# Queries and keys turned in 32x32 blocks on VectorE and gathered back from DRAM, in a hybrid attention decoder step

## The reference, cut to what matters

```python
h = rms_norm(x, norm_g); z = einsum('bsd,de->bse', h, w_in)     # one combined input projection
qa, ka, va, ga, qb, kb, vb, gb, ma, mb = split(z)
qa = rms_norm(qa per head of 64, q_norm_a); ka = rms_norm(ka, k_norm_a)   # the same for qb, kb
# A: 3 groups (window, dilation) = (128,1), (512,4), (2048,16), 8 heads each
scores = einsum('brnihd,brnjhd->brnhij', q, k) * d ** -0.5 + alibi ; out_g = softmax(scores) @ v
# B: 4 heads, two maps each: (softmax(s1) - lam * softmax(s2)) @ v
# gates, two branch projections, sigmoid merge, output projection, residual
# outputs too: the sampled window caches, shifted by 8 tokens, with the new rows behind
new_a{g}_sample = concat(cache_a{g}[:, 8:], new rows)
```

## Time and profile before

| | |
|---|---|
| Median of 3 runs | 1697.23 us (1694.59 to 1698.11) |
| The profiled execution's own time | 1693.59 us |
| Its span in the trace | 1691.7 us |
| PE busy | 1628.7 us, 96% |
| DVE, ACT, POOL busy | 719.9, 598.9, 665.4 us (43%, 35%, 39%) |
| Queue q1 (SyncE's), q10 (ScalarE's) | 221.68 MB, 112.22 MB |

### The profile page before, as it was taken

The page is one execution under the profiler, slowest core; times in us unless marked ns, Lnnn a source line. Parts: engine busy times, 40 slices in busy tenths (PEclk is TensorE's granted clock), DMA queues, the critical chain, the costliest instruction groups (busy, mean ns, idle before and its releaser), DMA issues.

```text
span 1691.7 us, 37775 instructions
## 1 busy us (share of the span) xinstructions
PE 1628.7 (96%) x14872; PEld 1394.2 (82%) x14872; DVE 719.9 (43%) x1788; ACT 598.9 (35%) x1405; POOL 665.4 (39%) x958
## 2 busy tenths in 40 slices
PE   7999999999999999999999999999899999999998
PEld 5787677878899999999999977788777788878787
DVE  6521576222372221722217544335354342588411
ACT  5422477222362221732218233334343344422300
POOL 5566120467433564535646221212221121565500
PEclk9999999999999999999999999999999999999999
DMA  5164810775516568155442879889898977865422
GB/s 166 54 236 154 260 50 13 229 241 185 180 44 212 191 219 282 43 183 195 155 128 67 298 268 325 276 290 349 262 309 297 323 258 234 285 204 176 135 94 81
DMA packets 184064, 336.30 MB, mean 199 GB/s; under 512 B 29969, under 2 KB 74130, under 8 KB 177746
## 3 DMA queue, kind: packets, MB, share of 16 engines
q1 hardware_dynamic: 143586, 221.68, 40.2%
q10 hardware_dynamic: 40304, 112.22, 19.9%
HBM read 294.05 MB, written 127.07 MB: 249 GB/s over the span
## 4 chain that ended last, share of the span: by engine, by line
PE 79%; DMA 6%; SPq 5%; DVE 3%; issue 3%; ACT 3%; POOL 2%; ACTq 0%; POOLq 0%; DVEq 0%
PE ps L2008 13%; PE ps L2010 13%; PE ps L2009 13%; PE ps L2167 4%; PE ps L2223 4%; PE ps L2065 4%; PE ps L2113 3%; PE ps L2066 3%; PE ps L2067 3%; PE ps L2187 3%; PE ps L2282 2%; DMA v_in<-in_cache_a_kv 2%; PE ps L2174 2%; DMA raw<-in_w_in 2%; PE ps L2134 2%
## 5 line engine op out<-in xcount | busy, mean ns | idle before, releaser
L993 POOL TENSOR_TENSOR w_lo<-raw,w_hi 128x512 fp32r<-128x512 f32 x140 | 181.2, 1300 | 424.2 <-ACT w_hi L1203 423.6
L2008 PE MATMUL ps<-w_hi,hT 128*128 128x512 f32 x824 | 339.6, 412 | 2.1 <-POOL hT L980 1.0
L2010 PE MATMUL ps<-w_hi,hT 128*128 128x512 f32 x824 | 330.1, 401 | 0.0
L2009 PE MATMUL ps<-w_lo,hT 128*128 128x512 f32 x824 | 329.7, 400 | 0.0
L2008 PEld LDWEIGHTS ps<-w_hi,hT 128*128 128x128 f32 x824 | 205.9, 250 | 21.4 <-DVE w_lo L1522 1.5
L2010 PEld LDWEIGHTS ps<-w_hi,hT 128*128 128x128 f32 x824 | 206.0, 250 | 20.3
L2065 PE MATMUL ps<-w_hi,hT 128*128 128x256 f32 x768 | 221.3, 288 | 1.2 <-issue 0.8
L2009 PEld LDWEIGHTS ps<-w_lo,hT 128*128 128x128 f32 x824 | 206.3, 250 | 18.1
L2066 PE MATMUL ps<-w_lo,hT 128*128 128x256 f32 x768 | 214.6, 279 | 1.0 <-issue 0.8
L2067 PE MATMUL ps<-w_hi,hT 128*128 128x256 f32 x768 | 214.1, 279 | 0.0
L1203 ACT ACTIVATE w_hi<-raw 128x512 fp32r<-128x512 f32 x158 | 98.9, 629 | 217.8 <-DMA raw<-in_w_in 198.6
(11 more groups left out here) (233 smaller groups left out, 2852.4 us busy)
## 6 DMA issues: line engine op xcount, KB each, us to landing
out<-in_cache_a_kv ACTq DMA_DIRECT2D x29, 2040.0 KB, 9.8
k_in<-in_cache_b_kv SPq DMA_DIRECT2D x128, 256.0 KB, 4.3
v_in<-in_cache_b_kv SPq DMA_DIRECT2D x128, 256.0 KB, 6.3
raw<-in_w_in SPq DMA_DIRECT2D x104, 256.0 KB, 4.1
k_in<-in_cache_a_kv SPq DMA_DIRECT2D x104, 256.0 KB, 7.0
v_in<-in_cache_a_kv SPq DMA_DIRECT2D x104, 256.0 KB, 7.3
out<-in_cache_a_kv ACTq DMA_DIRECT2D x7, 2016.0 KB, 8.7
raw<-in_w_in ACTq DMA_DIRECT2D x40, 256.0 KB, 5.6
```

The costliest lines, as they stand in the source:

```text
L993: pool.tensor_tensor(lo, raw_of(q), hi.bitcast(F32), ALU.subtract).then_inc(lo_done, 1)
L2008: pe.matmul(z, hi, wh, start=first, stop=False)
L2009: pe.matmul(z, hi, wl, start=False, stop=False)
L2010: return pe.matmul(z, lo, wh, start=False, stop=last)
```

## The change

Prompt queries and keys are no longer transposed on TensorE. VectorE transposes the 32x32 blocks of each tile within `zn` (queries) or from `kn` into `zn` (keys); SyncE stores the tile to a DRAM scratch `blocks_scr` and loads the whole of it back by 16 DMAs for each kind and group (`load_turned`), each of 32 partitions x 32 pieces of 32 floats (128 bytes), so that `qT` and `kT` come out as before. Query loads are issued two in each step of the k block, key loads three in each step of the v block from at_ = 1. Only the 64 sampled queries are still turned by TensorE (one turn in each k block). The score scale is now applied by GpSimd as it fills `qz`, and the register loop is unrolled. The 48 cache copies are all issued by SyncE: none in q and k blocks, 0, 5, 6, 6 in the v blocks (ahead of tile 8), 12, 8, 7, 4 in the attentions; each waits for the landing of the last but one. Their packets are 2048 and 2720 bytes. Some semaphores are shared to stay within their number.

```diff
-COPY_PARTS = ((0, 0, 120, 1536), (1, 0, 504, 1536)) + tuple((2, 510 * j, 510, 2720) for j in range(4))
-COPY_AT = (1, 2, 4, 6, 7)
+COPY_PARTS = ((0, 0, 120, 512), (1, 0, 504, 512)) + tuple((2, 510 * j, 510, 680) for j in range(4))
+COPIES_IN = (12, 8, 7, 4)
+COPIES_V = (0, 5, 6, 6)
...
+        def copied_at(j):
+            return (const_in, N_CONST + 16 * (j // 2 + 1)) if j % 2 else (copies, 16 * (j // 2 + 1))
...
+            def store_blocks(G, kind, i):
+                sp.wait_ge(turned, tile_turned(G, kind, i))
+                sp.dma_start(blocks_scr[G][kind == "k"][i * P:(i + 1) * P, :], zn[:, mi(G, kind, i) % 2, :])\
+                    .then_inc(blocks_sent(G, kind, i)[0], 16)
+            def load_turned(G, kind, part):
+                c, j = divmod(part, 4)
+                if part == 0:
+                    for i in range(NT - 2, NT):
+                        sp.wait_ge(*blocks_sent(G, kind, i))
+                    if kind == "q" and G:
+                        sp.wait_ge(o_out, stored(G - 1))
+                base = blocks_scr[G][kind == "k"][0:1, 0:1]
+                src = bass.AP(base.tensor, base.offset + c * P + 32 * j, [[CW, 32], [32 * CW, SEQ // 32], [1, 32]])
+                out = (kT if kind == "k" else qT)[32 * j:32 * j + 32, c * SEQ:(c + 1) * SEQ]
+                sp.dma_start(out.rearrange("p (b r) -> p b r", r=32), src).then_inc(kt_in if kind == "k" else qt_in, 16)
             def block_io(u):
...
                     if at_ < KC:
                         load_chunk(u + 1, at_)
+                    if kind in "qk" and i:
+                        store_blocks(G, kind, i - 1)
+                    if kind == "k" and i:
+                        for part in range(2 * i - 2, 2 * i):
+                            load_turned(G, "q", part)
+                    if kind == "v" and 0 < at_ < 7:
+                        for part in range(3 * at_ - 3, min(3 * at_, 16)):
+                            load_turned(G, "k", part)
...
+                    if kind == "v" and at_ >= NT - COPIES_V[G]:
+                        j = sum(COPIES_IN[:G]) + sum(COPIES_V[:G]) + at_ - NT + COPIES_V[G]
+                        if at_ < NT:
+                            copies_under_way(j, j + 1)
...
             def tables(G):
+                j0 = sum(COPIES_IN[:G]) + sum(COPIES_V[:G + 1])
+                share = COPIES_IN[G] // (2 if G == 0 else 3)
                 if G == 0:
-                    for j in range(len(COPY_AT)):
-                        copy_cache(sp, len(COPY_AT) + j)
                     for h in range(2, B_HEADS):
+                        copies_under_way(j0 + (h - 2) * share, j0 + (h - 1) * share)
                         sp.wait_ge(bs, 16 + 16 * (h - 1))
                         table_b(h)
...
+            def copies_under_way(j0, j1):
+                for j in range(j0, j1):
+                    if j == 0:
+                        sp.wait_ge(const_in, N_CONST)
+                    if j >= 2:
+                        sp.wait_ge(*copied_at(j - 2))
+                    copy_cache(sp, j)
...
+            def scaled(G, half, i, c):                              # GpSimd
+                rows, cols = slice(HD * half, HD * half + HD), slice(i * P, (i + 1) * P)
+                return pool.tensor_scalar(qz[rows, half, cols], qT[rows, c * SEQ + i * P:c * SEQ + (i + 1) * P],
+                                          qcol[rows, (0 if G else 1):(0 if G else 1) + 1], None, ALU.mult)
             def pad_first(G):
-                pool.wait_ge(t_ready, 17 * G + 17)
+                pool.wait_ge(turned, tile_turned(G, "k", NT - 1))
+                for i in range(NT - 2, NT):
+                    pool.wait_ge(*blocks_sent(G, "k", i))
...
-                pool.wait_ge(t_moved, 17 * G + 9)
+                pool.wait_ge(setup, 1)
+                pool.wait_ge(qt_in, 256 * (G + 1))
...
-                    if u and u != 2 and at_ in COPY_AT and len(COPY_AT) * (u - 1) + COPY_AT.index(at_) < N_COPIES:
-                        copy_cache(act, len(COPY_AT) * (u - 1) + COPY_AT.index(at_))
...
-                    if kind == "q" and i:
-                        move(G, "q", i - 1)
-                    if kind == "k" and i != 1:
-                        move(G, "q", NT) if i == 0 else move(G, "k", i - 2)
-                    if kind == "v" and at_ == 0:
-                        move(G, "k", NT - 1)
+                    if kind == "k" and i == 0:
+                        move(G)                                     # the sampled queries alone
...
+                        if kind == "q" and i < NT:                  # VectorE, behind zn
+                            dve.wait_ge(zn_ready, m + 1)
+                            dve.transpose(zn[:, m % 2, :], zn[:, m % 2, :]).then_inc(turned, 1)
+                        if kind == "k" and i:
+                            kk = TILES * G + i - 1
+                            dve.wait_ge(kn_ready, kk + 1)
+                            dve.transpose(zn[:, (m - 1) % 2, :], kn[:, kk % 3, :]).then_inc(turned, 1)
...
-                    if kind == "q" and i:                           # TensorE
-                        turn(G, "q", i - 1)
-                    if kind == "k" and i != 1:
-                        turn(G, "q", NT) if i == 0 else turn(G, "k", i - 2)
-                    if kind == "v" and at_ == 0:
-                        turn(G, "k", NT - 1)
+                    if kind == "k" and i == 0:
+                        turn_sample(G)
...
                 pe.wait_ge(v_ready, 9 * G + 8)
-                pe.wait_ge(t_moved, 17 * G + 17)
+                pe.wait_ge(t_moved, G + 1)
+                pe.wait_ge(kt_in, 256 * (G + 1))
```

More of the change, by code:

```diff
@@ L316, in build_step @@
         st_scr = [dram(f"st_scr{g}", [SEQ, 16]) for g in range(3)]
+        blocks_scr = [[dram(f"blocks_scr{g}{kind}", [SEQ, CW]) for kind in "qk"] for g in range(4)]
         os_scr = dram("os_scr", [2, DEC_B, ROW_C, P])
@@ L337, in build_step @@
         t_ready, t_moved = sem("t_ready"), sem("t_moved")
+        turned = sem("blocks_turned")
+        turn_out = [sem(f"blocks_out{s}") for s in range(2)]
+        qt_in, kt_in = sem("qT_in"), sem("kT_in")
         k_out = [sem(f"k_out{s}") for s in range(3)]
@@ L381, in build_step @@
         m_ready, m_t, m_hi, m_lo = sem("m_ready"), sem("m_t"), sem("m_hi"), sem("m_lo")
-        xl_in = [sem(f"xl_in{s}") for s in range(2)]
+        X_LOADS = [16 * len(range(s, TILES, 2)) for s in range(2)]
         yo_ready = sem("yo_ready")
@@ L393, in mi, with tile_turned, blocks_sent @@
             return 18 * G + (9 if kind == "k" else 0) + i
-        def ti(G, kind, i):
-            return 17 * G + (9 if kind == "k" else 0) + i
+        def tile_turned(G, kind, i):
+            return 16 * G + (8 if kind == "k" else 0) + i + 1
+        def blocks_sent(G, kind, i):
+            m = mi(G, kind, i)
+            return turn_out[m % 2], 16 * sum(x % 18 % 9 < NT for x in range(m % 2, m + 1, 2))
         def x_bank(j):
@@ L693, in copy_cache @@
             eng.dma_start(dst.rearrange("(m a x) -> a m x", a=16, x=piece),
-                          src.rearrange("(m a x) -> a m x", a=16, x=piece)).then_inc(copies, 16)
+                          src.rearrange("(m a x) -> a m x", a=16, x=piece)).then_inc(copied_at(j)[0], 16)
         block = ctx.enter_context(nc.Block())
@@ L881, in _ @@
                 if gg == -1:
[L882 removed]
+                    sp.wait_ge(first_in, 48)
             def gated(m):
@@ L952, in _ @@
                 sp.wait_ge(yo_out[s], 16 * 6)
-            sp.wait_ge(copies, 16 * N_COPIES)
+            for j in range(N_COPIES - 2, N_COPIES):
+                sp.wait_ge(*copied_at(j))
             for s in range(3):
@@ L1034, in block_ @@
                             G3, i3 = divmod(kk - 3, TILES)
-                            pool.wait_ge(t_ready, ti(G3, "k", min(i3, NT - 1)) + 1)
+                            pool.wait_ge(turned, tile_turned(G3, "k", min(i3, NT - 1)))
                             if k_sent[kk % 3][kk - 3]:
@@ L1068, in pad_queries @@
                             pool.wait_ge(aq, 16 + 64 * (G - 1) + 16 * (c - 1) + 2 * i + 2)
-                            cols = slice(i * P, (i + 1) * P)
-                            src = slice(c * SEQ + i * P, c * SEQ + (i + 1) * P)
-                            copied(qz[0:HD, 0, cols], qT[0:HD, src])
-                            copied(qz[HD:P, 1, cols], qT[HD:P, src]).then_inc(qz_ready, 1)
+                            scaled(G, 0, i, c)
+                            scaled(G, 1, i, c).then_inc(qz_ready, 1)
                     return
-                with pool.Fori(0, NC - 1) as c:
+                for c in range(1, NC):
                     for s, i in enumerate(TILE_ORDER):
-                        wait_reg(pool, bq, 16 + 16 * c + 2 * s + 2)
-                        cols = slice(i * P, (i + 1) * P)
-                        pool.tensor_copy(qz[0:HD, 0, cols], qT[0:HD, ds((c + 1) * SEQ + i * P, P)])
```

(23 more changed lines are left out.)

64 lines of the change are left out of this document (25 added, 39 removed).

## The result

The kernel after takes 1723.83 us (median of 4 runs, 1721.41 to 1727.47) against 1696.82 us for the kernel before (4 runs beside it): a ratio of 1.0152, interval 1.0133 to 1.0171, 27 us or 1.5% slower. The forecast was slower at 1703 us, with a range of 1675 to 1739. The profiled execution took 1722.63 us, its span 1720.6.

A forecast was written before the change was run, and what follows sets the result against it. TensorE, busy for 96% of the span, was taken as the bound. Turns -32, v blocks +37 and k blocks +1 gave +6 on the profiled 1693.6, so 1699.6; on the median 1703 us, range 1675 to 1739.

The forecast's parts named there:

- What it removes: Q and k blocks: sixteen prompt turns a group leave TensorE, 0.45 or 0.55 us each, 32 us in all.
- What it adds at no cost: VectorE's 64 block transposes (43 us) and GpSimd's scaled copies stay hidden; at most 5 us would show in block u = 0.
- The k blocks: Chunk-fetch round with store and query loads takes 11.0 to 11.5 us against 11.2 for two tiles; 1 us on TensorE.
- The v blocks: Key loads, chunks and copies in SyncE's one queue delay keys and last chunk at the A attentions; 37 us on TensorE.
- The prices: DMA in the v blocks: full copy 6.0 us, small copy a quarter, key load 1.1, chunk or 256 KB table 0.7.
- so 37: Start of the A attentions: 40 us of lateness less four units' scores already done, 1 us a group, leaves TensorE 37.
- The lateness: Last chunk of the v blocks against its due time: 6.3, 17.4 and 16.7 us late in G = 1 to 3, 40 summed.
- The credit of 3 us: Start of the A attentions: TensorE has four units' scores done while the last chunk is late, 1 us for each group.
- the forecast's own case: Whole kernel slower by +3.4 to +25 us, 1700.6 to 1722, likeliest 1703; chance 0.35.
- All hidden: V blocks: queue not served in order or chunks come around the copies; -32 + 1, 1666 us; chance 0.08.
- The queue drains faster: V blocks: copies and loads some 9 us shorter over three groups; -22 to -3.4 us, middle 1684; chance 0.27.
- Small packets dear: V-block loads at the upper end or the 512-byte price, 1.9 us each; over +25 us, middle 1739; chance 0.17.

The follow-up runs named there:

- e2: Kernel after, but the 48 copies as in the kernel before (large packets, in the blocks, on ScalarE's queue, five by SyncE in G = 0): 1768.97 us, ratio 1.0408.
- e10: Kernel after with four copies in each v block of G = 1 to 3, the other five issued by ScalarE in q blocks: 1690.57 us, ratio 0.9951.
- e8: Kernel after with key loads reading the same bytes in 4 KB rows instead of 128-byte pieces (scores not the reference's): 1690.26 us, ratio 0.9963.
- e1: Kernel after with the 17 cache copies of the v blocks left out, so part of the shifted caches isn't written: 1669.93 us, ratio 0.9839.
- e7: Kernel after with the v-block copies in the same steps, issued by ScalarE on its own queue: 1717.75 us, ratio 1.0119.
- e9: Kernel after with 10, 62 and 62 unused matmuls before TensorE's wait for the keys in G = 1 to 3: 1721.81 us, ratio 1.0142.
- e5: Kernel after with the 17 v-block copies moved to the q blocks of G = 1 to 3, on ScalarE's queue: 1669.09 us, ratio 0.9833.
- e4: Kernel after with the cache copies in the large packets of the kernel before (6144 and 10880 bytes): 1725.31 us, ratio 1.0176.
- e6: Kernel after with each v block's copies all issued behind its last chunk and last key load: 1727.76 us, ratio 1.0177.
- e11: The kernel before, unchanged, run once more for a second profile: 1699.25 us (one run).

## Why the prediction came out as it did

**What it removes: right, a little less.** Of L1977's 272 transposes the 16 of the sampled queries are left, the q and k tiles follow each other every 5.6 us, and the blocks give -29.5 us where the sum had -32 for the turns and +1 for the k blocks.

**What it adds at no cost: right.** VectorE's 64 transposes and GpSimd's scaling show nowhere on TensorE's side; the attention of G = 0 took 114.1 us in both traces, with no gap. The longest wait for `zn` is 0.9 us, at the turn of the sampled queries of G = 0, where the sum allowed up to 5.

**The k blocks: right for this kernel, by a narrow margin.** TensorE's waits for `zn` in all blocks come to 1.4 us. The margin is what e2 used up: with copies beside the rounds the blocks were 73 us longer. The prediction's round left out that `zn` also waits for its stored blocks to land; that cost nothing here and is in e2's waits.

**The v blocks: the mechanism right.** One queue, SyncE's order, the last chunk ahead of the first exponential, and the gate of the keys. Of TensorE's idle time 6, 17 and 17 us were named as the sign; measured 6.3, 19.8 and 16.0. The prices hold: by the landings of the copies a whole step of G = 2 took 10.5 to 10.9 us where the prices give 6.0 + 3.3 + 0.7 and half a value tile, 10.35; a copy was 5.8 us at the margin (e10), and three key loads in long rows made the step 2.6 to 2.7 us shorter (e8). The distance between landings of key loads is no such evidence, though the prediction named it as its sign: it was 0.6 to 1.6 us, 1.0 in the mean, in G = 2 of the kernel after, and 1.0 in the mean in e8 too, where the loads were cheaper.

**The step that was off: the loss of TensorE for each group, "so 37".** The three attentions were 51.6 us longer. Three terms make the difference.

- *The lateness was sized too small.* The first exponential comes 9.0, 22.6 and 17.9 us behind the block's last product, and 1.1 where it is on time (e1). That is 7.9, 21.5 and 16.8 us late, 46 in sum, where the sum had 6.3, 17.4 and 16.7, together 40. Most is in G = 2: three kept value tiles stand ahead of its last chunk in SyncE's issues (at 630.94, 652.68 and 668.73), 2.1 us at the sum's own price, and the sum counts kept values in G = 3 alone.
- *The credit of 3 us, "TensorE has four units' scores done by then", was nearly nothing.* The same ten scores stand ahead of the first transposition in e1, where nothing is late. That transposition came 7.4, 21.1 and 16.8 us later than in e1: 45 of the 46 us reached it.
- *The clock had no term.* Behind the first transposition the three attentions took 65.7, 54.2 and 62.3 us, in e1 64.0, 51.7 and 60.2: 6.2 us more. In exactly these stretches the granted clock stood at one half (1.2 GHz) for 3.4, 5.2 and 4.4 us, and in e1 for none. So each us at 1.2 GHz cost about half a us. In e7, e8, e9 and e10 the same stretches held 6.4, 7.0, 14.5 and 14.4 us at one half and were 2.7, 3.0, 7.0 and 6.8 us longer than e1's, 0.4 to 0.5 for each us again. The Trainium skill (TensorE: Matmul & The Clock Gate) describes, in its Part 1, an array that falls to the lower clock when it has been idle. The trace agrees: the granted clock fell within these waits or within 0.6 us behind them, and in e9 it fell over the second one, of 6.9 us in G = 2. That these 6.2 us are the clock's is worked out from rows and agrees over five runs; no run undid it.

The first scores, too, ran at the lower clock (3.2, 3.3 and 2.5 us for ten, in e1 2.2, 2.3 and 1.9), but this cost nothing that shows: the wait for the exponential came behind them, and in e9, where they were faster, it was longer.

**The rest of the distance to 1703.** The sum gave +6 on the span, the stages give +20 without the sampled one (-29.5 + 51.6 - 2.0). Of the 14 between them 6 are lateness, 2 the credit, 6 the lower clock and 1.5 the smaller gain in the blocks, less the 2 of the last row; about half a us is left. The medians differ by 27, 7 us more than these stages. That is the +9.0 of the sampled stage less some 2, since the profiled execution of before was further below its median (3.2 us) than that of after (1.2). In e1 the same sum of stages gives -31 and the ratio -27. Whether the turning lengthens the sampled stage by a few us stays open: three profiles with turns on TensorE have a mean of 470.7 us, ten with the turning 473.9, and single executions of either spread over some 8 us and more. So the time ended 2 us above the forecast's own case (+3.4 to +25) and inside the range for reasons of which only the queue's part was foreseen.

**The rivals.** All hidden is what e1 and e5 would be, not this kernel. "The queue drains faster" failed, since it did not. "Small packets dear" put the loads at 1.9 us each, and the time landed in its bracket (over +25) without its mechanism: in the full queue a load of 128-byte pieces was 0.9 us dearer than one of 4 KB rows, and the steps fit the sum's own 1.1 us. The Trainium skill (DMA: Bandwidth & Descriptors, its opening table) wants 512 bytes for line rate: by e8 the direction holds, small pieces cost, though less than the price of as many 512-byte packets. For the cache copies the size (2 to 10.9 KB) made no difference (e4).

**What the change was worth.** One part of it, the turning, is a gain of 27 us (e1, e5); the other, the copies, was put into the one kind of block that the first had filled. e6 and e7 show that neither order nor a second queue mends that, and e5 shows that another block does.

## What to carry to other kernels

Work that leaves the bound engine for DMA brings transfers with a due time. Before placing it, add up for each stage between producer and gate what the 16 engines must move, from measured prices: here 16 loads of 1.1, nine of 0.7 and a copy of 6 each, in 50 us less the start. Transfers that nobody waits for then go into the stages with room left, and when such a stage is full, reordering it or giving it a second queue only picks another consumer to be late.

## What the runs showed of the hardware

- With some 10 us of transfers outstanding on its queue SyncE stood in its issues: three loads of 1024 pieces took 8.7 and 9.6 us to issue in the v block of G = 2, single ones up to 4.5 us, while 3.4 us sufficed for three earlier in the block. The same loads in 32 rows of 4 KB took at most 1.1 us each in the same block (e8).
- A DRAM to DRAM copy of 2.09 MB costs about 5.8 us at the margin (e10), in packets of 2720 bytes or of 10880 (e4: same attentions within 2 us).
- 128 KB from DRAM to SBUF in 1024 pieces of 128 bytes is 0.9 us dearer in a full queue than in 32 rows of 4 KB (0.57 over all 48 loads); both landed about 1 us apart, so the distance of landings did not tell the price.
- After a wait of 15 us the first ten scores took 3.28 us; with the wait filled by other matmuls 1.92 us. Each us of half clock (1.2 GHz) in stretches that TensorE bounds cost 0.4 to 0.5 us (after, e7 to e10).
- The sampled stage of one and the same kernel took 466.6 and 474.5 us in two executions, with 3.4 and 13.7 us at half clock within it. The length doesn't follow this time alone: 13.7 us at half clock went with 474.5 us in one kernel (e11) and 470.8 in another (e4). What brings these short dips was not found.
